# Self-attention's heads placed between the half-slots of the memory value projection

## The reference, cut to what matters

```
y    = rmsnorm(x, norm_mix_g) @ w_in
q, k = partial_rotary(y[..., 0:512]), partial_rotary(y[..., 512:1024])   # 8 heads of 64
v    = y[..., 1024:1536]
att  = dilated_sliding_attention(q, k, v)            # 3 patterns, one softmax over 256 keys
conv = silu(layernorm(depthwise_conv31(a * sigmoid(g))))   # 512 channels
h    = x + concat(att, conv) @ w_out
mn   = rmsnorm(mem, norm_mem_g)
xk, xv = mn @ w_xk, mn @ w_xv                        # 256 memory rows, used after h
```

## Time and profile before

| what | value |
|---|---|
| time, median of 3 runs | 1476.51 us (1467.35 to 1479.66) |
| time of the profiled execution | 1470.95 us |
| its span | 1468.9 us |
| PE busy | 1394.6 us, 95% |
| DVE busy | 1085.5 us, 74% |
| ACT busy | 830.9 us, 57% |
| chain that ended last | PE 83%, DVE 13%, ACT 2% of the span |

### The profile page before, as it was taken

The page is one execution under the profiler, slowest core; times in us unless marked ns, Lnnn a source line. Parts: engine busy times, 40 slices in busy tenths (PEclk is TensorE's granted clock), DMA queues, the critical chain, the costliest instruction groups (busy, mean ns, idle before and its releaser), DMA issues.

```text
span 1468.9 us, 21894 instructions
## 1 busy us (share of the span) xinstructions
PE 1394.6 (95%) x8175; PEld 1218.4 (83%) x8175; DVE 1085.5 (74%) x1571; ACT 830.9 (57%) x1150; POOL 56.1 (4%) x60
## 2 busy tenths in 40 slices
PE   5997899999999999999999998998999999999997
PEld 5795587989988988899999997777888888888886
DVE  4989565655557876755555788767898898898896
ACT  4444453543445754444333575445787787787784
POOL 0000000000002130000000013010000000000000
PEclk9999899999999999999999999998999999999999
DMA  8544042555554520455555451117998998988982
GB/s 299 177 151 163 0 145 87 176 196 181 192 189 129 168 77 1 132 166 190 181 192 183 129 184 39 37 65 289 398 352 302 348 340 310 372 318 306 373 317 116
DMA packets 162963, 292.75 MB, mean 199 GB/s; under 512 B 6832, under 2 KB 78924, under 8 KB 162764
## 3 DMA queue, kind: packets, MB, share of 16 engines
q1 hardware_dynamic: 162336, 291.08, 57.4%
q10 hardware_dynamic: 556, 0.67, 0.1%
HBM read 290.69 MB, written 1.05 MB: 199 GB/s over the span
## 4 chain that ended last, share of the span: by engine, by line
PE 83%; DVE 13%; ACT 2%; issue 1%; DMA 1%; ACTq 0%; SPq 0%; POOL 0%; DVEq 0%
PE bank L537 23%; PE bank L539 23%; PE bank L538 23%; DVE weights_split L1915 4%; DVE arena L2100 3%; PE bank L1199 2%; PE bank L1002 1%; PE bank L1274 1%; PE bank L1008 1%; PE bank L993 1%; PE bank L671 1%; PE bank L651 1%; PE bank L1020 1%; PE bank L1251 1%; DMA weights<-in_w_in_dram 1%
## 5 line engine op out<-in xcount | busy, mean ns | idle before, releaser
L1915 DVE TENSOR_TENSOR weights_split<-weights,weights_split 128x1024 fp32r<-128x1024 f32 (+4 forms) x266 | 304.4, 1187 | 168.8 <-ACT weights_split L1427 168.7
L1427 ACT ACTIVATE weights_split<-weights 128x1024 fp32r<-128x1024 f32 (+4 forms) x266 | 258.5, 1022 | 285.9 <-PE bank L539 283.2
L537 PE MATMUL bank<-features_split,weights_split 128*128 128x256 f32 x912 | 263.2, 289 | 15.2 <-DVE features_split L1942 5.4
L538 PE MATMUL bank<-features_split,weights_split 128*128 128x256 f32 x912 | 260.8, 286 | 0.0
L539 PE MATMUL bank<-features_split,weights_split 128*128 128x256 f32 x912 | 260.7, 286 | 0.0
L537 PE MATMUL bank<-weights_split,features_split 128*128 128x512 f32 (+3 forms) x560 | 217.5, 388 | 8.5 <-DVE features_split L1922 3.6
L539 PE MATMUL bank<-weights_split,features_split 128*128 128x512 f32 (+3 forms) x560 | 214.0, 382 | 0.0
L538 PE MATMUL bank<-weights_split,features_split 128*128 128x512 f32 (+3 forms) x560 | 213.8, 382 | 0.0
L537 PEld LDWEIGHTS bank<-features_split,weights_split 128*128 128x128 f32 x912 | 177.7, 195 | 18.8 <-DVE weights_split L1915 6.2
L538 PEld LDWEIGHTS bank<-features_split,weights_split 128*128 128x128 f32 x912 | 177.9, 195 | 0.5
L539 PEld LDWEIGHTS bank<-features_split,weights_split 128*128 128x128 f32 x912 | 177.8, 195 | 0.0
(11 more groups left out here) (374 smaller groups left out, 2250.9 us busy)
## 6 DMA issues: line engine op xcount, KB each, us to landing
weights<-in_moe_gate_dram SPq DMA_DIRECT2D x26, 1024.0 KB, 6.8
weights<-in_moe_up_dram SPq DMA_DIRECT2D x24, 1024.0 KB, 7.0
weights<-in_moe_down_dram SPq DMA_DIRECT2D x24, 1024.0 KB, 7.3
weights<-in_w_in_dram SPq DMA_DIRECT2D x20, 1024.0 KB, 5.2
weights<-in_w_up_dram SPq DMA_DIRECT2D x16, 1024.0 KB, 5.2
weights<-in_w_down_dram SPq DMA_DIRECT2D x16, 1024.0 KB, 4.9
weights<-in_w_out_dram SPq DMA_DIRECT2D x12, 1024.0 KB, 4.9
weights<-in_ffn_gate_dram SPq DMA_DIRECT2D x11, 1024.0 KB, 5.3
```

The costliest lines, as they stand in the source:

```text
L537: pe.matmul(ps, lhs(0), rhs(0), start=start, stop=False, skip_group_check=shared)
L538: pe.matmul(ps, lhs(0), rhs(1), start=False, stop=False, skip_group_check=shared)
L1427: do(act.activation(split_flat(j)[:, 0, part], raw_flat(j)[:, part], ACT.Copy), "hi", j, b)
L1915: do(dve.tensor_tensor(split_flat(j)[:, 1, part], raw_flat(j)[:, part], split_flat(j)[:, 0, part].bitcast(F32), ALU.subtract), "lo", j)
```

## The change

The attention of the first block is put between the parts of the xv slots.

- PE: the fourth slot of xk moves behind the turning of queries and keys. The four xv slots are no longer worked off ahead of the attention. Each is cut in two parts, one for each half of the memory rows (12 matmuls of 512 columns), and part s is done at the end of step s of the attention, for s from 0 to 7 (`cross_values`). Banks are opened in the new order.
- ACT: `first_attention` takes the place of `attention` here. In step s it first splits the high part of a slot (s = 2, 4, 6, 8), copies the turned probabilities of head s-1, makes the exponentials of head s, then waits for the reciprocal and scales the probabilities itself (two `Copy` activations with a scale; they were DVE's), and copies a finished xv bank out (s = 3, 4, 7, 8).
- DVE: of the 62 rounds of taps 23 are moved into the attention and one stands just ahead of it. Each step has one round between the maximum and the reciprocal and one or two at its end. The low part of a slot stands in the even steps, the split of a pair of heads in the odd ones. The last rounds are done in steps 8 and 9, behind the split of the last pair. Ahead of the memory's norm two rounds are taken out, and behind its turned rows four are put in.

```diff
--- before.py
+++ after.py
@@ -704,10 +704,8 @@
                 turn_norm(1)
                 tokens_out("v", HT, 512)
                 pe.wait_ge(*after("ht", 1))
-                for i in range(4):
+                for i in range(3):
                     features_out("xk", MT, "xk", i)
-                for i in range(2):
-                    tokens_out("xv", MT, 512, i)
                 pe.wait_ge(*after("rotated"))
                 for b in range(4):
                     ps = open_bank("qkT", b)
@@ -716,8 +714,27 @@
                             mm = pe.transpose(ps[:, c * S + t * P:c * S + (t + 1) * P],
                                               QK[:, t, (2 * b + c) * P:(2 * b + c + 1) * P], ident)
                     mm.then_inc(*cpe.mark("filled", "qkT", b))
+                features_out("xk", MT, "xk", 3)
                 pe.wait_ge(*after("read", "qkT", 3))
                 pe.wait_ge(*after("read", "v", 0, 1))
+                cross_slot = {}
+
+                def cross_values(s):
+                    if s >= 8:
+                        return
+                    i, r, t = s // 4, s // 2 % 2, s % 2
+                    if t == 0:
+                        cross_slot[i, r] = weights("xv")
+                    j, w = cross_slot[i, r]
+                    ps = open_bank("xv", i, t) if r == 0 else bank_of["xv", i, t]
+                    for k in range(4):
+                        mm = matmul3(ps[:, :], lambda z: MT[:, z, 4 * r + k, t * P:(t + 1) * P],
+                                     lambda z: w[:, z, k, :], r == 0 and k == 0, r == 1 and k == 3)
+                    if r == 1:
+                        mm.then_inc(*cpe.mark("filled", "xv", i, t))
+                        cpe.also("slot", j)
+                    elif t == 1:
+                        mm.then_inc(*cpe.mark("slot", j))
 
                 def scores1(h, ps):
                     o = 64 * (h % 2)
@@ -726,7 +743,7 @@
                                        QKT[o:o + HD, 4 + h // 2, :], start=True, stop=True)
                     return mm
 
-                attention(0, AH, scores1, pair_outs("att_o", (), V))
+                attention(0, AH, scores1, pair_outs("att_o", (), V), between=cross_values)
 
                 def mean_over_channels(name, need, src):
                     pe.wait_ge(*after(need))
@@ -1485,6 +1502,23 @@
                                           bias=NM[:, u % 3, t:t + 1], accum_out=DEN[:, u % 3, t:t + 1]),
                            "exp", u, t)
 
+                def first_attention(heads, ahead, between):
+                    for s in range(heads + 1):
+                        ahead(s)
+                        if s >= 1:
+                            act.wait_ge(*after("pt", s - 1))
+                            if s >= 3:
+                                act.wait_ge(*after("o", s - 3))
+                            do(act.activation(flat(PT[:, (s - 1) % 2]), PT_BANK[(s - 1) % 2][:, 0:TT * S], ACT.Copy),
+                               "pt_copied", s - 1)
+                        if s < heads:
+                            exps(s, False)
+                            act.wait_ge(*after("rden", s))
+                            for t in range(TT):
+                                do(act.activation(PR[:, s % 3, t, :], PR[:, s % 3, t, :], ACT.Copy,
+                                                  scale=RDEN[:, s % 3, t:t + 1]), "probs", s)
+                        between(s)
+
                 def attention(u0, heads, between=lambda s: None, until_now=False, ahead=lambda s: None):
                     n = P + S if until_now else TT * S
                     for s in range(heads + 1):
@@ -1532,17 +1566,25 @@
                 high(2)
                 for t in range(TT):
                     copy_out(V[:, t, :], psum("v", 0, t)[:, :], "v", 0, t)
-                for i in range(4):
+                for i in range(3):
                     high(1)
                     copy_out(XKT[:, 2 * i:2 * i + 2, :], two(psum("xk", i)), "xk", i)
-                for i in range(2):
-                    high(2)
-                    for t in range(TT):
-                        copy_out(XV[:, t, i * 512:(i + 1) * 512], psum("xv", i, t)[:, :], "xv", i, t)
                 act.wait_ge(*after("heads_selected"))
                 for b in range(4):
                     copy_out(QKT[:, 2 * b:2 * b + 2, :], two(psum("qkT", b)), "qkT", b)
-                attention(0, AH)
+                copy_out(XKT[:, 6:8, :], two(psum("xk", 3)), "xk", 3)
+                high(1)
+
+                def next_slot(s):
+                    if s in (2, 4, 6, 8):
+                        high(1)
+
+                def cross_values(s):
+                    if s in (3, 4, 7, 8):
+                        i, t = s // 4 - (s % 4 == 0), 1 - s % 2
+                        copy_out(XV[:, t, i * 512:(i + 1) * 512], psum("xv", i, t)[:, :], "xv", i, t)
+
+                first_attention(AH, next_slot, cross_values)
 
                 act.wait_ge(*after("read", "cmean"))
                 do(act.activation(SIG[:, :, :], C[:, :, :], ACT.Square), "csq")
@@ -2115,9 +2157,10 @@
                 for i in range(4):
                     if i == 2:
                         rows_norm(1, MEM)
-                    conv_taps(4 if i < 2 else 2)
+                    conv_taps(3 if i < 2 else 2)
                     low(1)
                 turned(1, "norm_mem_g", 0, MT, T1)
+                conv_taps(4)
                 for _ in range(2):
                     low(1)
                     conv_taps(2)
@@ -2137,10 +2180,9 @@
                 own()
                 do(dve.tensor_tensor(x1, r[0], r[1], ALU.subtract))
                 do(dve.tensor_tensor(x2, r[2], r[3], ALU.add), "rotated")
-                for i in range(8):
+                for i in range(3):
                     low(1)
-                    conv_taps(5 if i < 6 else 4)
-                assert taps_done == [TAPS, TAPS]
+                    conv_taps(4)
 
                 def outs1(h):
                     if h % 2:
@@ -2168,7 +2210,25 @@
                     dve.wait_ge(*after("csilu"))
                     split(lambda z: CAT[:, z, 4:8, :], C[:, :, :], "convT")
 
-                attention(0, AH, 0.125, flat(logc), outs1)
+                conv_taps(1)
+                for s in range(AH + 2):
+                    if s < AH:
+                        dve.wait_ge(*after("scores", s))
+                        if s >= 3:
+                            dve.wait_ge(*after("pt", s - 3))
+                        do(dve.scalar_tensor_tensor(flat(PR[:, s % 3]), SC_BANK[s % 2][:, :], 0.125, flat(logc),
+                                                    ALU.mult, ALU.add), "scores_read", s)
+                        own()
+                        do(dve.tensor_reduce(NM[:, s % 3, :], PR[:, s % 3], AX.X, ALU.max, negate=True), "negmax", s)
+                        conv_taps(1)
+                        dve.wait_ge(*after("exp", s, 1))
+                        do(dve.reciprocal(RDEN[:, s % 3, :], DEN[:, s % 3, :]), "rden", s)
+                    if s in (0, 2, 4, 6, 8):
+                        low(1)
+                    if s >= 3 and s % 2:
+                        outs1(s - 2)
+                    conv_taps(2 if s % 2 else 1)
+                assert taps_done == [TAPS, TAPS]
                 conv_mean()
                 conv_variance()
                 conv_scaled()
```

## The result

| kernel | median | span of the profiled run | ratio to before, 95% interval |
|---|---|---|---|
| before | 1471.18 us (1466.9 to 1479.66, 13 runs) | 1468.9 us | |
| changed | 1461.54 us (1458.05 to 1471.04, 13 runs) | 1458.3 us | 0.9931 (0.9909 to 0.9953) |

The change is faster by 0.7%, 9.6 us between the medians and 10.6 us between the two profiled spans. The forecast was 7.7 us of gain and a time of 1466.0 us, which is 4.5 us above the measured median. PE is still the bound: 1390.4 us busy, 95% of the span. In the chain that ended last DVE's share fell from 13% to 9% and PE's rose from 83% to 87%, which fits the stretch of taps that went under PE's work.

A forecast was written before the change was run, and what follows sets the result against it. PE bounds the kernel, but ahead of the heads DVE's low parts and taps do. Sums 9.6 us earlier less 1.9 for the clock give 7.7 us gain; 1466.0 us named between 1463.25 and 1468.8, range 1456 to 1477.

The forecast's parts named there:

- the mark: Forecast: start of the channel sums, 172.17 us before; measured: mean square behind w_out's stage, DVE's first instruction on `norm_stats`.
- The front: Ahead of the heads: first scores read at 112.6 us, first exponentials at 115.35 behind ACT's queue, four added rounds hidden.
- A table load with a drain: First exponentials: a rule adding about 1.4 us of drain to the load, making the gain 6.3 us; the forecast rejected it.
- DVE's steps: Inside the heads on DVE: an even step takes 5.73 us, an odd one 5.05 us.
- The free round: On DVE between scores and reciprocal: a 0.79 us round of taps costs nothing, the way stays 2.57 us.
- PE's step: Inside the heads on PE: turning, values, scores and half an xv slot sum to 5.43 us a step.
- misfit: Over the eight heads: 0.7 us added for PE and DVE running nearly level, with 0 to 4 us possible.
- rival B: In the heads: DVE and PE don't mesh, 0.5 us lost a head, gain 4.4 us, time 1469.3 us; chance 0.17.
- The end: Behind the last head: PE waits 1.4 us, then 3 us for the last taps; sums begin at 162.55 us.
- The clock: Behind the new 3 us idle ahead of the channel sums: PE's clock falls, costing 1.9 us, between 0 and 5.5.
- rival C: In the heads: the low clock takes hold, up to 36 us lost, time 1502 us, slower than before; chance 0.05.
- rival D: Slots 15 to 19: later low parts delay loads of slots 18 to 22, gain lost, about 1473.7 us; chance 0.08.

The follow-up runs named there:

- s_same: The changed kernel unaltered, profiled once more; one run, span 1462.9 us.
- s_again: The changed kernel unaltered, timed on the same chip as g_again; median 1463.83 us, ratio to before 0.9944.
- c_scores_twice: The changed kernel with the scores of heads 1 and 2 computed twice on PE, to fill its idle gaps; ratio to before 0.9936.
- b_taps_early: The changed kernel with three more rounds of taps ahead of the first head, none left for steps 8 and 9; ratio to before 0.9916.
- h_filler_tail: The changed kernel with six filler matmuls on V ahead of the sums over channels; one run, mean square at 197.75 us.
- f_both: b_taps_early with slot 15's split moved behind head 0 on ACT and its low part into step 1 on DVE; ratio to before 0.9877.
- g_all: f_both with slot 19's split behind the last turned head's copy, its low part behind the subtraction of the channels' mean; ratio to before 0.9870.
- d_taps_ahead: The changed kernel with all taps done ahead of the first head, as before the change; ratio to before 1.001.
- g_again: g_all once more, timed on the same chip as the unaltered changed kernel; median 1454.19 us, ratio to before 0.9880.
- a_dve_scales: The changed kernel with DVE instead of ACT scaling the probabilities, as before the change; median 1467.88 us, ratio to before 0.9970.

## Why the prediction was right

The mechanism was right: each step was met closely, in place and in size. That the mark came 7.85 us earlier, where 7.7 was forecast, is in part luck, since two clock terms cancelled.

- *The front.* First scores at 112.6, measured 112.59 in the changed kernel's first profile. Hundredths are luck: in s_same and s_again they came at 110.93 and 110.86, because there the clock did not fall between 70 and 80 us (granted 1.00, against 0.83 before and in the first profile). ACT's queue of a copy, a split and a table load was the limit, with exponentials at 115.33 (115.35 forecast). The four rounds behind the memory's norm were hidden, and of the 4.48 us of idle time there 1.34 are left.
- *A table load with a drain* (the Trainium skill, "ScalarE: Activation LUTs", section "What ACT_TABLE_LOAD costs"), which would have made the gain 6.3 us, is not seen: the load starts at 114.04, right behind ACT's split, and takes 1.28 us, and the exponential starts at 115.33. The measured time decides.
- *DVE's steps.* 5.73 and 5.05 us were forecast. s_same has 5.69 where nothing waits (133.15 to 138.84) and 5.02 (128.13 to 133.15). The free round and the 0.37 us of waiting are there.
- *PE's step.* 5.43 us was forecast. Heads are turned every 5.60 us in s_same, s_again, c_scores_twice and b_taps_early. The part of an xv slot was the mis-sized term: from the end of a head's values to the next scores pass 2.94 us, not 2.79 (142.30 + 1.01 to 146.25). The first matmul of a stream is 0.34 us ahead of the second, where the others are 0.23 apart (143.30, 143.64, 143.87), and from the last to the scores it is 0.32. An uncut slot of 24 pays that once, and here every 12 do. PE is thus the bound by 0.2 us a step, not level with DVE. The 0.7 us that had been added for misfit nearly covered it (in s_same the sums begin 50.11 us after the first scores, 0.86 more than the 49.25 without it), and rival B (0.5 us a head) fell.
- *The end.* The split of slot 19, the wait of 1.19 us (1.4 forecast) and the 3 us for the last taps (3.05 measured) came as worked out. With the misfit I had 49.95 us from the first scores to the sums; s_same and s_again have 50.1. b_taps_early shows that the wait was real and avoidable.
- *The clock.* I expected one fall, behind the 3 us, for 1.9 us. It came in all profiles with that wait, and h_filler_tail puts it at 1.7 to 2.2. But I had let the low stretch of the kernel before at 189 us go on. After the first fall it did not recur in the changed kernel, which gave 1.6 us back. And in the first profile there was another fall in the heads, which cost 1.6. So: 9.6 forecast ahead of clock terms, measured 7.88 at the sums (the heads' fall), less 1.63 up to the last half of w_out, plus 1.60 behind it, makes the 7.85 us. Without the fall in the heads, as in s_same and s_again, the way from the first scores to the mark is 1.0 and 1.6 us shorter.
- *The time.* The forecast of 1466.0 us named the middle between two starting points, the profiled run of before and a median of three that lay 5.6 us above it. The median of 13 runs of before is 1471.18 us, next to the profiled run. That middle made 2.8 of the 4.5 us by which the time was missed, and the gain, larger than forecast (9.6 us between the medians), the rest.
- *Slower cases.* The low clock never held on in the heads (rival C), and the later low parts delayed no slot (rival D): the last half of w_out waits for 2.10 us as before. The gain stayed below 1%, as forecast, though 13 runs tell it from none.

## What to carry to other kernels

Where an in-order engine holds long work that nobody waits for (here 24 rounds of taps), that work can be laid in its waits and under the bound engine's work, in pieces no longer than the wait that covers them. Look then at both ends: three rounds left over at the end cost 3.05 us and a low stretch of the clock, while the same engine sat idle 2.78 us at the front. And what stands in front of the first and the last link of a chain is paid for, where in the middle it can be hidden. Taking a split of 1.9 us from the first link brought the sums 1.3 us forward (f_both), and from the last 1.5 us (g_all), while the splits in steps 2, 4 and 6 left PE's pace at 5.60 us. The table load at the front was not moved in any run.

## What the runs showed of the hardware

- Whether PE's clock falls behind a short idle time is not settled by the program. The same gaps of 1.02 and 1.23 us brought a fall once in five profiles. The gap of 2.10 us ahead of the last half of w_out brought one in the kernel before, d_taps_ahead, g_all and g_again, and none in b_taps_early, f_both and h_filler_tail. The wait of 3.05 us brought one in all four profiles that had it (changed, s_same, s_again, c_scores_twice; one of 4.72 us did in a_dve_scales), and then none followed at the 2.10.
- One such fall costs 1.6 to 2.6 us: the stage from the sums to the mean square takes 35.6 us without one, and 37.2 to 38.2 with.
- The runs of the changed kernel lie 13 us apart, and the longest of them has the lowest mean of the granted clock: 1471.04 us at 0.976, while the shortest has 1458.05 us at 0.988. In the traces the code behind the mark, the same in all, differs by 7.3 us between executions, with PE's busy time 6.5 us apart.
